# One stage for latent keys, values and queries, with the norm weights folded into the down projections

## The chip, the cores and the metric

One core of one Trainium2 chip runs the whole program. The time is device microseconds of one execution, and the median of three runs is what two versions are compared by. The core has five engines with instruction queues of their own: TensorE (PE; its weight loads are PEld), VectorE (DVE), ScalarE (ACT), GpSimd (POOL) and SyncE (SP, which here only issues DMAs). An engine takes its instructions strictly in order and waits on semaphores for the others.

## The reference, cut to what matters

The program is two layers of a small transformer (512 tokens and 16 meta tokens, width 1024, all in float32), followed by two further layers of other kinds. The change is in the second layer's latent attention, between the first layer's mixture of experts and the attention itself:

```python
def shared_latent_kv(h, kv_norm, w_dkv, kv_lat_norm, w_uk, w_uv, cos, sin):
    c = jnp.einsum('bld,dr->blr', rmsnorm(h, kv_norm), w_dkv)       # 1024 -> 256 + 64
    c_kv = rmsnorm(c[..., :KV_LORA_RANK], kv_lat_norm)
    k_rope = apply_rope(c[..., KV_LORA_RANK:], cos, sin)
    k_nope = jnp.einsum('blr,rhd->blhd', c_kv, w_uk)
    v = jnp.einsum('blr,rhd->blhd', c_kv, w_uv)
    return k_nope, k_rope, v

def mla_mixer(hn, w_dq, q_norm, w_uq, ...):                          # hn = rmsnorm(h, b_norm)
    cq = rmsnorm(jnp.einsum('bld,dr->blr', hn, w_dq), q_norm)        # 1024 -> 384
    q = jnp.einsum('blr,rhd->blhd', cq, w_uq)                        # 8 heads x (128 + 64)
    q_nope = q[..., :QK_NOPE_DIM]
    q_rope = apply_rope(q[..., QK_NOPE_DIM:], cos[:, None, :], sin[:, None, :])
```

Both norms are taken of the same `h`; they differ only in the weight that each column is multiplied by (`kv_norm`, `b_norm`).

## The kernel before

**Arithmetic.** Every large product is made of three matmuls of rounded halves (`products`, lines 105 to 109): the high part of one operand with both parts of the other, and the low part with the high one. An operand is split by a copy on ScalarE that rounds (the "high" part) and a subtraction on VectorE (the "low" part).

**Weights.** All weights come in chunks of up to 128 x 2048, in one list. SyncE loads them in that order into raw buffers (four outside the experts, `load_chunk`), each as soon as the buffer's last user is done; ScalarE (`split_high`, line 246) and VectorE (`split_low`, line 260) split them into one of three pairs of split buffers, once the chunk that had the pair is used up. The list is mixed with chunks for the third part of the network, the "ada" pieces (`load_list`): 1 MB each, two of them make one `ada_rows` of 16 matmuls on TensorE, read from the raw buffer without a split, followed by `ada_pick` on VectorE. Six of these pieces, (1,0) to (1,5), stand behind the first experts' last chunk and ahead of the latent stage's first.

**The stages here** are `moe` 0, `latent`, `query`, `attend`. A stage starts on an engine once all engines have ended the stage ahead; only `route`, `latent` and `enter` start without that.

`latent`: GpSimd fetches the experts' rows (`yc`, five DMAs, four of 1 MB). Per tile t of 128 tokens (four, and a fifth of the 16 meta tokens), VectorE adds the two expert rows (`combine_vector`), ScalarE takes the root of the mean square, VectorE multiplies by its reciprocal and the row of weights (line 339), TensorE transposes (line 357), ScalarE and VectorE split the result into `x_high` and `x_low`. Three `ada_rows` stand between these transposes. Then the chunks c, c+1 and c+2 are split and TensorE makes `c` (five tiles of 24 matmuls, 320 wide); ScalarE copies it out (`c_rows`), the norm over 256 and the rotation by position are made on VectorE for all tiles; ten small transposes and five of the rotary part follow (lines 999 and 1000), split into `ck_high`, `ck_low`, `k_rope_high`, `k_rope_low`; then come the keys (96 matmuls of 264) and the values (60 of 512).

`query`: `h` is normed, transposed and split a second time, with the row `b_norm`; `cq` (96 matmuls of 384), its norm over 384 (line 1201), transposes (line 1136), split; the rotary queries (36 matmuls of 512), their rotation on VectorE (six operations a tile, lines 948 to 956, two buffers in turn), transposes (line 1151), split; the plain queries `q_nope`, eight heads of nine matmuls of 512, copied out by ScalarE (line 1189).

`attend` begins on TensorE with ten matmuls whose result nobody reads (line 1292), then the first scores, then ten more (line 1296).

## Time and profile before

| | us |
|---|---|
| median of three runs | 2884.91 |
| lowest and highest of them | 2884.13, 2894.32 |
| the profiled execution's own time | 2893.18 |
| its span in the trace | 2891.4 |
| granted TensorE clock, mean over the span | 0.927 of full |

A granted clock of 1.00 is 2.4 GHz, one of 0.50 is 1.2 GHz; a value between is a stretch with some of both. A DMA's landing, a wait or a busy time of the trace belongs to the one profiled execution, which took 8.27 us more than the median.

### The profile page before, as it was taken

The page shows a single profiled execution, that of the slowest core. Times are in us where ns is not written, and L with a number is a line of the kernel's source. Part 1 is how long each engine was busy: PE and PEld are TensorE (multiplying, and loading weights), DVE is VectorE, ACT ScalarE, POOL GpSimd, SP SyncE. Part 2 cuts the span into 40 slices and gives each one's busy share as a digit, 9 for nine tenths or more (in the row PEclk, how much of TensorE's full clock was granted, in tenths as well). Part 3 has the DMA queues.
Part 4 walks back from the last instruction along what each step waited for, and adds up shares of the span by engine and source line. Part 5 has one row for each costly group of instructions (what it writes and reads, how often), then busy time and mean ns, then how long its engine had stood idle before and what let it go on. Part 6 is the DMA issues. An engine that isn't in the chain of part 4 may idle for free.

```text
span 2891.4 us, 31119 instructions
## 1 busy us (share of the span) xinstructions
PE 2566.1 (89%) x11522; PEld 2033.9 (70%) x11522; DVE 1874.9 (65%) x2237; ACT 1366.2 (47%) x1901; POOL 211.8 (7%) x221
## 2 busy tenths in 40 slices
PE   5879999778996999997987889989798998899997
PEld 2668888566775888884665667778666666688886
DVE  4679999644635999985863756545774664644356
ACT  2258888533633888884522322123332563332321
POOL 1022222100001222211000000000000000000000
PEclk9789999888997999998996889999998899899999
DMA  7379991431013999615220245443211002222230
GB/s 259 112 300 365 367 361 69 174 115 46 16 44 131 369 365 367 251 63 212 73 73 29 80 165 199 149 142 116 74 60 44 1 1 102 80 102 102 73 110 29
DMA packets 100374, 418.57 MB, mean 145 GB/s; under 512 B 25737, under 2 KB 26081, under 8 KB 60785
## 3 DMA queue, kind: packets, MB, share of 16 engines
q1 hardware_dynamic: 70976, 373.27, 35.5%
q0 software_dynamic: 29248, 43.32, 4.2%
q8 instruction: 93, 1.52, 0.2%
q14 instruction: 57, 0.46, 0.1%
HBM read 484.91 MB, written 48.76 MB: 185 GB/s over the span
## 4 chain that ended last, share of the span: by engine, by line
PE 74%; DVE 15%; ACT 5%; issue 3%; DMA 2%; POOL 0%; SPq 0%; DVEq 0%; ACTq 0%; POOLq 0%
PE psum L107 22%; PE psum L108 21%; PE psum L109 21%; PE psum L742 2%; DVE w_low L260 2%; ACT w_high L246 1%; PE psum L1532 1%; DVE ada_sum L1564 1%; PE psum L486 1%; PE psum L357 1%; DVE rg_in L2181 1%; DMA raw<-in_ada 1%; DVE gla_head L2181 1%; PE psum L759 1%; DMA rows<-in_rows 1%
## 5 line engine op out<-in xcount | busy, mean ns | idle before, releaser
L260 DVE TENSOR_TENSOR w_low<-raw,w_high 128x2048 fp32r<-128x2048 f32 (+1 forms) x216 | 485.3, 2258 | 260.2 <-ACT w_high L246 247.9
L246 ACT ACTIVATE w_high<-raw 128x2048 fp32r<-128x2048 f32 (+1 forms) x216 | 405.7, 1886 | 317.6 <-PE psum L109 304.2
L107 PE MATMUL psum<-x_high,w_high 128*128 128x512 f32 x848 | 348.4, 411 | 39.6 <-DVE w_low L260 25.3
L108 PE MATMUL psum<-x_high,w_low 128*128 128x512 f32 x848 | 339.6, 400 | 0.0
L109 PE MATMUL psum<-x_low,w_high 128*128 128x512 f32 x848 | 337.8, 398 | 0.0
L107 PE MATMUL psum<-w_high,mlp_high 128*128 128x512 f32 x512 | 205.1, 401 | 27.5 <-DVE mlp_low L932 11.5
L107 PEld LDWEIGHTS psum<-x_high,w_high 128*128 128x128 f32 x848 | 160.6, 189 | 87.2 <-issue 40.4
L109 PE MATMUL psum<-w_low,mlp_high 128*128 128x512 f32 x512 | 205.3, 401 | 0.0
L108 PE MATMUL psum<-w_high,mlp_low 128*128 128x512 f32 x512 | 204.9, 400 | 0.0
L107 PE MATMUL psum<-w_high,xg_high 128*128 128x512 f32 x480 | 195.7, 408 | 6.2 <-DVE xg_low L853 6.2
L108 PEld LDWEIGHTS psum<-x_high,w_low 128*128 128x128 f32 x848 | 160.5, 189 | 43.7 <-issue 6.4
L260 DVE TENSOR_TENSOR w_low<-raw_extra,w_high 128x2048 fp32r<-128x2048 f32 x78 | 177.8, 2289 | 18.5 <-ACT w_high L246 13.4
L109 PE MATMUL psum<-w_low,xg_high 128*128 128x512 f32 x480 | 189.4, 394 | 0.0
L108 PE MATMUL psum<-w_high,xg_low 128*128 128x512 f32 x480 | 189.3, 394 | 0.0
L109 PEld LDWEIGHTS psum<-x_low,w_high 128*128 128x128 f32 x848 | 160.5, 189 | 39.3 <-issue 1.1
L246 ACT ACTIVATE w_high<-raw_extra 128x2048 fp32r<-128x2048 f32 x78 | 149.7, 1919 | 15.0 <-PE psum L109 15.0
L107 PEld LDWEIGHTS psum<-w_high,mlp_high 128*128 128x128 f32 x512 | 98.9, 193 | 50.3 <-ACT mlp_high L928 17.1
L107 PE MATMUL psum<-w_high,x_high 128*128 128x512 f32 (+5 forms) x272 | 104.3, 383 | 33.5 <-DVE w_low L260 16.5
L893 POOL DMA_INDIRECT expert_rows<-yb,table x80 | 92.5, 1156 | 549.4 <-PE psum L742 444.9
L928 ACT ACTIVATE mlp_high<-mlp_square 128x512 fp32r<-128x512 f32 x64 | 40.5, 632 | 190.1 <-DVE mlp_square L2533 190.1
L1532 PE MATMUL psum<-raw,condition 128*128 128x512 f32 x192 | 95.0, 653 | 31.7 <-DMA raw<-in_ada 30.2
L853 DVE TENSOR_TENSOR xg_low<-psum,xg_high 128x1024 fp32r<-128x1024 f32 x80 | 98.0, 1224 | 30.1 <-ACT xg_high L799 21.6
(542 smaller groups left out, 5410.4 us busy)
## 6 DMA issues: line engine op xcount, KB each, us to landing
raw<-in_moe SPq DMA_DIRECT2D x138, 1024.0 KB
raw_extra<-in_moe SPq DMA_DIRECT2D x102, 1024.0 KB
raw<-in_mlp SPq DMA_DIRECT2D x64, 1024.0 KB
raw<-in_ada SPq DMA_DIRECT2D x48, 1024.0 KB
rows<-in_rows POOLq DMA_DIRECT2D x20, 512.0 KB, 4.7
raw<-in_evin SPq DMA_DIRECT2D x10, 1024.0 KB
raw<-in_foxqk SPq DMA_DIRECT2D x8, 1024.0 KB
xn_rows<-xn_tiles POOLq DMA_DIRECT2D x9, 512.0 KB, 3.0
```

The source lines that it names most:

```text
L107: pe.matmul(out, ah, bh, start=first, stop=False)
L108: pe.matmul(out, al, bh, start=False, stop=False)
L109: return pe.matmul(out, ah, bl, start=False, stop=last)
L246: act.activation(k.WH[k.W_AT[c]][:, 0:w], k.RAW[k.RAW_AT[c]][:, 0:w], ACT.Copy).then_inc(*k.A.step("high", c))
L260: dve.tensor_tensor(wl[:, 0:w], k.RAW[k.RAW_AT[c]][:, 0:w], wh[:, 0:w].bitcast(F32), ALU.subtract).then_inc(*k.V.step("low", c))
L357: mm = pe.transpose(k.PS[:, b, i * P:(i + 1) * P], xn, const(k, "ident"))
L742: mm = pe.transpose(flat(k, f * P, f * P + P), k.XG[:, j % XG_SLOTS, f * P:(f + 1) * P], const(k, "ident"))
L853: dve.tensor_tensor(k.XGL[j % 2][:, :, :].rearrange("p a b -> p (a b)"), flat(k, 0, D), k.XGH[j % 2][:, :, :].rearrange("p a b -> p (a b)" ...
L893: pool.indirect_dma_start(k.y_d[:, :], bass.IndirectOffsetOnAxis(ap=k.TAB[:, 2 * j + 1:2 * j + 2], axis=0), k.YB[:, j % 2, :], None, bound ...
L928: act.activation(dst, src, ACT.Copy).then_inc(*k.A.step(*label))
L1532: mm = pe.matmul(k.PS[:, bank, :], k.CS[:, f:f + 1].to_broadcast([P, P]), w[:, i * ADA_COLS:(i + 1) * ADA_COLS], start=(f == 0), stop=(f = ...
L2181: f(*a, **b).then_inc(*V.step())
```

## The change

The stage `query` is gone; `latent` makes keys, values and queries.

- One normalisation: `h` is multiplied by the reciprocal root alone, without a row of weights, by a `tensor_scalar`. Its transposed halves serve both down projections.
- The weights `kv_norm` and `b_norm` go into the four chunks of the down projections when these are split (`GAINED`): four ScalarE copies with a scale per partition instead of one copy, four VectorE operations (raw times scale minus high) instead of one subtraction. Only the 1280 used columns of the key chunks are split, not 2048. The scales are columns, transposed with the other gain rows in the first stage (11 rows instead of 9); the two rows are no longer loaded as rows of 128 partitions.
- The chunks are in the order of the new stage: both down projections, keys, rotary queries, values, plain queries.
- The six ada pieces stand behind c and c+1 in the list of loads; c and c+1 are split before the norm.
- TensorE's order: `c`, `cq`, the transposes of both, keys, rotary queries, values, transposes of rotary queries, plain queries. `cq` keeps banks 0 to 3 of PSUM, `c` and its transposes 4 to 7. The rotated rows have four buffers instead of two. ScalarE copies out all values.
- ScalarE splits two chunks of `attout`'s weights in this stage, c+9 and c+10, instead of one.
- `ada_pick` of the first vector writes its unused product to PSUM instead of SBUF.

```diff
@@ load_list
-        follow.setdefault(k.MOE0[n // 6] + 3 * NBLK - 1, []).append((1, n))
+        follow.setdefault((k.FIRST[("latent",)] + 1, k.MOE0[1] + 3 * NBLK - 1)[n // 6], []).append((1, n))
@@ split_high
+        if c in k.GAINED:
+            g, f0, w = k.GAINED[c]
+            for i in range(4):
+                act.activation(wh[:, i * w:(i + 1) * w], raw[:, i * w:(i + 1) * w], ACT.Copy,
+                               scale=k.GAINC[:, g, f0 + i:f0 + i + 1]).then_inc(*k.A.step("high", c))
+            continue
@@ split_low
+                dve.scalar_tensor_tensor(out=wl[:, part], in0=k.RAW[k.RAW_AT[c]][:, part], scalar=k.GAINC[:, g, f0 + i:f0 + i + 1],
+                                         in1=wh[:, part].bitcast(F32), op0=ALU.mult, op1=ALU.subtract).then_inc(*k.V.step("low", c))
@@ norm_vector
+            dve.tensor_scalar(xn, k.H[:, t, :], k.RS[:, t:t + 1], None, ALU.mult).then_inc(*k.V.step(name, "xn", t))
@@
+LATENT_ORDER = (0, 1, 4, 5, 2, 6, 3, 7, 8)
@@ latent_tensor
+    for q in range(2):
+        wh, wl = chunk_pair(k, pe, c + 2 + q)
+        for t in range(XT):
+            for f in range(4):
+                w = slice(f * QR, f * QR + QR)
+                mm = products(pe, k.PS[:, t, 0:QR], k.XH[:, 4 * q + f, t * P:(t + 1) * P], k.XL[:, 4 * q + f, t * P:(t + 1) * P],
+                              wh[:, w], wl[:, w], q == 0 and f == 0, q == 1 and f == 3)
...
+    for t in range(XT):
+        pe.wait_ge(*k.after("cq normed", t))
+        for f in range(3):
+            mm = pe.transpose(k.PS[:, t, f * P:(f + 1) * P], k.CQN[:, t, f * P:(f + 1) * P], const(k, "ident"))
@@ latent_scalar
+    split_high(k, act, c + 1)
     norm_scalar(k, act, "latent", range(XT + 1), "pair", k.SQ, "combined", 0)
-    split_high(k, act, c + LOOK)
+    split_high(k, act, c + 2)
...
+    split_high(k, act, c + 9)
+    for h in range(HEADS):
+        if h == 4:
+            split_high(k, act, c + 10)
+        act.wait_ge(*k.after("qn", h))
+        act.activation(k.QN[:, h, :], k.PS[:, latent_bank(LATENT_QN + h), :], ACT.Copy).then_inc(*k.A.step("qn out", h))
@@ latent_vector
+    split_low(k, dve, c + 1)
+    norm_vector(k, dve, "latent", range(XT + 1), "pair", None, combined)
...
+    split_low(k, dve, c + 4)
     dve.wait_ge(*k.after("cq root"))
@@ stage_list
-    return ([("pool",), ("route", 0, XT + 1), ("moe", 0), ("latent",), ("query",), ("attend",), ("attout",),
+    return ([("pool",), ("route", 0, XT + 1), ("moe", 0), ("latent",), ("attend",), ("attout",),
@@ chunk_list
+        if st[0] == "latent":
+            new = [new[i] for i in LATENT_ORDER]
```

SyncE's queue between the last chunk of the first experts and the latent stage (`in_kv`, `in_q` and `in_wo` are weights, `in_ada` the ada pieces, `raw_49` to `raw_52` the four raw buffers), before:

```order
L231 DMA raw_50<-in_moe 128x2048
L218 DMA raw_51<-in_ada 128x4x512
L218 DMA raw_52<-in_ada 128x4x512
L218 DMA raw_49<-in_ada 128x4x512
L218 DMA raw_50<-in_ada 128x4x512
L218 DMA raw_51<-in_ada 128x4x512
L218 DMA raw_52<-in_ada 128x4x512
L234 DMA raw_49<-in_kv 128x2048
L234 DMA raw_50<-in_kv 128x2048
```

and now:

```order
L232 DMA raw_50<-in_moe 128x2048
L235 DMA raw_51<-in_kv 128x2048
L235 DMA raw_52<-in_kv 128x2048
L219 DMA raw_49<-in_ada 128x4x512
L219 DMA raw_50<-in_ada 128x4x512
L219 DMA raw_51<-in_ada 128x4x512
L219 DMA raw_52<-in_ada 128x4x512
L219 DMA raw_49<-in_ada 128x4x512
L219 DMA raw_50<-in_ada 128x4x512
L235 DMA raw_51<-in_q 128x1536
L235 DMA raw_52<-in_q 128x1536
```

Two weight chunks have moved ahead of the six ada pieces, and pieces (1,2) and (1,3) now take the buffers of these two chunks, so they are issued once VectorE has split them.

TensorE's queue behind the last matmul of `c` (320 wide), before:

```order
L108 MATMUL psum<-w_high_55,x_low 16x320
L109 MATMUL psum<-w_low_58,x_high 16x320
L999 MATMUL psum<-const,c_norm 128x128 x2
L1000 MATMUL psum<-const,k_rope_rows 128x128
L999 MATMUL psum<-const,c_norm 128x128 x2
```

and now behind the last matmul of `cq` (384 wide):

```order
L108 MATMUL psum<-w_high_54,x_low 128x384
L109 MATMUL psum<-w_low_57,x_high 128x384
L1084 MATMUL psum<-const,c_norm 128x128 x2
L1085 MATMUL psum<-const,k_rope_rows 128x128
L1084 MATMUL psum<-const,c_norm 128x128 x2
```

The same transposes stand in the same order, but behind `cq`, which is made in between. Where they end, at the tile of the meta tokens, TensorE's queue now goes on so:

```order
L1085 MATMUL psum<-const,k_rope_rows 128x128
L1084 MATMUL psum<-const,c_norm 128x16 x2
L1085 MATMUL psum<-const,k_rope_rows 128x16
L1089 MATMUL psum<-const,cq_norm 128x128 x12
L107 MATMUL psum<-ck_high,w_high_55 128x264
L108 MATMUL psum<-ck_high,w_low_58 128x264
```

The twelve transposes of the queries' latents (`cq_norm`) have moved in between the keys' transposes and the keys' matmuls (264 wide).

ScalarE's queue at the end of the queries, `q_nope` being their copies and `q_high` the first instruction of `attend`, before:

```order
L928 ACTIVATE q_rope_high<-psum 128x4x128 x4
L246 ACTIVATE w_high_53<-raw_49 128x1536
L1189 ACTIVATE q_nope<-psum 128x512 x4
L246 ACTIVATE w_high_55<-raw_50 128x2048
L1189 ACTIVATE q_nope<-psum 128x512 x4
L928 ACTIVATE q_high<-q_nope 128x512
```

and now:

```order
L949 ACTIVATE q_rope_high<-psum 128x4x128 x4
L254 ACTIVATE w_high_55<-raw_50 128x2048
L1208 ACTIVATE q_nope<-psum 128x512 x4
L254 ACTIVATE w_high_53<-raw_51 128x2048
L1208 ACTIVATE q_nope<-psum 128x512 x4
L949 ACTIVATE q_high<-q_nope 128x512
```

A second weight split (`raw_51`, chunk c+10) stands between the copies of heads 0 to 3 and those of heads 4 to 7. It waits until TensorE has used up chunk c+8 in the same pair of buffers, that is, until all heads are made.

## Rows read from the trace of the kernel before

**Rows 1.** the page's part 4, shares of the chain that ended last

```profile
PE 74%; DVE 15%; ACT 5%; issue 3%; DMA 2%; POOL 0%; SPq 0%; DVEq 0%; ACTq 0%; POOLq 0%
```

**Rows 2.** windows: length; busy (count) of PE, PEld, DVE, ACT, POOL; clock, DMA share, GB/s

```profile
549.00:558.70 9.70, 2.12 (x5) 0.58 (x4) 2.59 (x3) 0.20 (x1) 3.37 (x7) 0.84 0.99 391
594.20:614.60 20.40, 20.37 (x120) 18.84 (x120) 4.60 (x3) 2.84 (x5) 0.00 (x0) 0.86 0.34 116
614.60:622.90 8.30, 0.03 (x1) 0.07 (x1) 4.58 (x14) 5.06 (x13) 0.00 (x0) 0.64 0.00 0
622.90:627.40 4.50, 3.19 (x15) 2.75 (x15) 4.31 (x11) 2.37 (x10) 0.00 (x0) 0.50 0.29 79
627.40:640.30 12.90, 12.83 (x94) 12.86 (x95) 3.03 (x7) 3.02 (x8) 0.00 (x0) 0.87 0.09 35
640.30:654.60 14.30, 14.30 (x64) 10.21 (x62) 6.54 (x7) 5.72 (x8) 0.00 (x0) 1.00 0.36 128
654.60:667.60 13.00, 6.02 (x34) 5.52 (x33) 9.99 (x15) 9.38 (x19) 0.00 (x0) 0.76 0.01 2
667.60:686.40 18.80, 18.80 (x98) 18.49 (x96) 3.14 (x3) 3.84 (x9) 0.00 (x0) 0.89 0.18 57
686.40:692.10 5.70, 2.74 (x14) 2.12 (x13) 4.67 (x8) 4.21 (x8) 0.00 (x0) 0.70 0.00 0
692.10:702.10 10.00, 10.00 (x38) 8.08 (x38) 5.95 (x15) 0.00 (x0) 0.00 (x0) 0.83 0.31 105
702.10:708.90 6.80, 2.69 (x18) 2.21 (x17) 5.88 (x15) 1.68 (x3) 0.00 (x0) 0.77 0.00 0
708.90:727.30 18.40, 18.40 (x73) 14.45 (x71) 5.38 (x5) 7.85 (x10) 0.00 (x0) 0.90 0.30 97
```

**Rows 3.** chain of waits in order of time: start us, us, what

```profile
549.17 9.49 DMA yc<-expert_rows
...
562.88 1.30 DVE h L920
...
566.76 1.30 DVE xn L339
...
588.76 0.89 PE psum L357 x8
...
591.78 2.30 DVE w_low L260
```

**Rows 4.** timeline, VectorE: start us, us, what [idle before it]

```profile
555.86 2.60 DVE L920 SCALAR_TENSOR_TENSOR h<-yc,gate,h 128x1024 f32<-128x1024 f32 x2 [14.69 <-DMA yc<-expert_rows]
...
618.34 2.07 DVE L1094 SCALAR_TENSOR_TENSOR c_norm<-c_rows,rs,param 128x256 f32<-128x256 f32 x5
...
625.03 0.42 DVE L932 TENSOR_TENSOR ck_low<-psum,ck_high 128x256 fp32r<-128x256 f32 x1
...
687.60 2.19 DVE L1201 SCALAR_TENSOR_TENSOR cq_norm<-psum,rs,param 128x384 f32<-128x384 f32 x4
689.71 1.75 DVE L260 TENSOR_TENSOR w_low<-raw,w_high 128x1536 fp32r<-128x1536 f32 x1
...
696.00 0.42 DVE L948 TENSOR_TENSOR rotate_c<-psum,const 128x256 f32<-128x256 f32 x1 [2.68 <-PE psum L109]
```

**Rows 5.** groups by shape, VectorE, 1290 to 1360 us

```profile
L1743 DVE TENSOR_SCALAR h<-h,rs 128x1024 f32<-128x1024 f32 x4 | 3.0, 753 | 0.1
```

**Rows 6.** timeline, SyncE's queue: first issue, us to the last

```profile
535.86 15.66 SPq L218 DMA_DIRECT2D raw<-in_ada  x3
...
574.85 14.26 SPq L234 DMA_DIRECT2D raw<-in_kv  x4
```

**Rows 7.** timeline, ScalarE and TensorE at the stage's end

```profile
719.55 1.91 ACT L246 ACTIVATE w_high<-raw 128x2048 fp32r<-128x2048 f32 x1
...
727.46 0.60 ACT L1189 ACTIVATE q_nope<-psum 128x512 f32<-128x512 f32 x1 [1.50 <-PE psum L109]
...
728.10 2.55 PE L1292 MATMUL psum<-q_rope_high 128*128 128x512 f32 x10 [0.69 <-ACT q_nope L1189]
```

More of the change, by code:

```diff
@@ L316, in norm_vector @@
 def norm_vector(k, dve, name, tiles, mode, gain, earlier=None):
-    dve.wait_ge(*k.after("row", gain))
+    if gain:
+        dve.wait_ge(*k.after("row", gain))
     def lows(t):
@@ L962, in table3, with key_col, latent_bank, latent_freed @@
     return k.CONST[:, at + t0 * h:at + (t0 + nt) * h].rearrange("p (t f) -> p t f", t=nt)
+def key_col(t):
+    return (META + t * P, P) if t < XT else (0, META)
+LATENT_KV = 2 * HEADS
+LATENT_QR = LATENT_KV
+LATENT_V = LATENT_QR + XT
+LATENT_TURN = LATENT_V + 2 * (XT + 1)
+LATENT_QN = LATENT_TURN + XT
+def latent_bank(n):
+    return 4 + n % 4 if n < 8 else n % 8
+def latent_freed(n):
+    if n < LATENT_KV:
+        return "kv out", n
+    if n < LATENT_V:
+        return "qr rotated", n - LATENT_QR
+    if n < LATENT_TURN:
+        return "kv out", n - XT
+    if n < LATENT_QN:
+        return "qr lo", n - LATENT_TURN
+    return "qn out", n - LATENT_QN
+def kv_place(k, r):
+    n = r if r < LATENT_KV else r + XT
+    if r < 2 * HEADS:
+        h, s = divmod(r, 2)
+        return k.KT[:, h, s * KHALF:(s + 1) * KHALF], k.PS[:, latent_bank(n), 0:KHALF]
+    t, half = divmod(r - 2 * HEADS, 2)
+    if t < XT:
+        return k.VAL[:, t, half * HALF:(half + 1) * HALF], k.PS[:, latent_bank(n), :]
+    return k.H[0:META, XT, half * HALF:(half + 1) * HALF], k.PS[0:META, latent_bank(n), :]
 def latent_tensor(k, pe, *_):
     c = k.FIRST[("latent",)]
+    def bank(n):
+        if 4 <= n < 8:
+            pe.wait_ge(*k.after(*latent_freed(n - 4)))
+        elif 8 <= n < 12:
+            pe.wait_ge(*k.after("cq lo", n - 8))
+        elif n >= 12:
+            pe.wait_ge(*k.after(*latent_freed(n - 8)))
+        return latent_bank(n)
     for t in range(XT + 1):
@@ L1099, in latent_vector @@
     dve.tensor_copy(k.KRD[:, :, ROPE:P], k.KRD[:, :, 0:ROPE]).then_inc(*k.V.step("k turned by position"))
-    split_low(k, dve, c + 3)
-    for t in range(XT + 1):
-        c0, n = key_col(t)
-        dve.wait_ge(*k.after("kr", t))
-        low(k, dve, k.KRL[:, c0:c0 + n], k.PS[:, t % 4, 2 * P:2 * P + n], k.KRH[:, c0:c0 + n], "kr lo", t)
-        src = k.PS[:, t % 4, 0:2 * P].rearrange("p (a c) -> p a c", a=2)[:, :, 0:n]
-        low(k, dve, k.CKL[:, :, c0:c0 + n], src, k.CKH[:, :, c0:c0 + n], "ck lo", t)
@@ L1192, in query_vector @@
-def query_vector(k, dve, *_):
-    c = k.FIRST[("query",)]
-    norm_vector(k, dve, "query", range(XT), "pair", "b_norm")
-    split_low(k, dve, c + LOOK)
+    split_low(k, dve, c + 4)
     dve.wait_ge(*k.after("cq root"))
@@ L1218, in query_vector @@
         cols = slice(t * P, (t + 1) * P)
[L1219 to L1220 removed]
+        low(k, dve, k.QRTL[:, :, cols], turned_queries(k, t), k.QRTH[:, :, cols], "qr lo", t)
     dve.wait_ge(*k.after("qn", 3))
[L1222 removed]
+    split_low(k, dve, c + 9)
+    dve.wait_ge(*k.after("qn", 7))
+    split_low(k, dve, c + 10)
 def unit(u):
@@ L2942, in place_rest @@
     k.CKL = k.at("ck_low", [P, 2, KEYS], k.end, F32R)
-    k.CQN = k.at("cq_norm", [P, XT, QR], k.SCR)
+    k.CQN = k.at("cq_norm", [P, XT, QR], va)
+    k.SQQ = k.at("cq_squares", [P, QR], k.end)
     k.QRTH = k.at("q_rope_high", [P, HEADS // 2, SEQ], k.XHAT, F32R)
@@ L3032, in place_rest @@
     k.OL = k.at("fox_low", [P, DK, SEQ], fv, F32R)
-SCALAR = {"pool": pool_scalar, "route": route_scalar, "moe": moe_scalar, "latent": latent_scalar, "query":
-          query_scalar, "attend": attend_scalar, "attout": attout_scalar, "enter": enter_scalar,
+SCALAR = {"pool": pool_scalar, "route": route_scalar, "moe": moe_scalar, "latent": latent_scalar, "attend": attend_scalar, "attout": attout_scalar, "enter": enter_scalar,
           "even_in": even_in_scalar,
@@ L3063, in chunk_list @@
     out, moe0, overflow = [], [], {}
-    names = {"pool": ["a_w"], "latent": ["kv"], "query": ["q"], "attout": ["wo"], "even_in": ["evin", "evz"],
+    names = {"pool": ["a_w"], "latent": ["kv", "q"], "attout": ["wo"], "even_in": ["evin", "evz"],
              "even_out": ["evout"], "fox_in": ["foxqk", "foxf", "foxv"], "fox_out": ["foxg", "foxout"]}
@@ L3098, in program @@
     k.high_next = k.low_next = 0
+    c = first.get(("latent",), 0)
+    k.GAINED = {c: (9, 0, CWID), c + 1: (9, 4, CWID), c + 2: (10, 0, QR), c + 3: (10, 4, QR)} if c else {}
     k.xn_d = nc.dram_tensor("xn_rows", ((XT + 1) * P, D), F32, kind="Internal").ap()
@@ L3246, in rows @@
                 k.row_next += 1
-                if ("row done", ROWS[r]) not in marks and marks.get("complete"):
+                if ROWS[r] not in COLUMNS_ONLY and ("row done", ROWS[r]) not in marks and marks.get("complete"):
                     break
-                if r >= ROW_SLOTS:
-                    pool.wait_ge(*k.after("row done", ROWS[r - ROW_SLOTS]))
+                if ROWS[r] in COLUMNS_ONLY:
+                    continue
+                prev = next((p for p in range(r - ROW_SLOTS, -1, -ROW_SLOTS) if ROWS[p] not in COLUMNS_ONLY), None)
+                if prev is not None:
+                    pool.wait_ge(*k.after("row done", ROWS[prev]))
                 pool.dma_start(k.ROWB[:, r % ROW_SLOTS, :], dram["rows"][r]).then_inc(
```

267 lines of the change are left out of this document (128 added, 139 removed).

## The prediction, made before the changed kernel ran

> **What bounds the kernel now.** I read the shares of the chain that ended last first: TensorE holds 74% of it, VectorE 15% [rows 1], so time is won where TensorE stands still or runs at half clock. Then I cut the latent and query stages into windows at the places where TensorE changes work [rows 2]. Each row is one piece of work or one pause; the clock behind the busy times tells how much of it ran at 2.4 GHz. Where TensorE is busy throughout, length times clock is the length at full clock: `c` 20.4 x 0.86 = 17.5 us, `cq` 18.8 x 0.89 = 16.7, keys 12.9 x 0.87 = 11.2, values 14.3, rotary queries 10.0 x 0.83 = 8.3, plain queries 18.4 x 0.90 = 16.6. The rest is pauses: 8.3 and 4.5 us around the keys' norm and transposes, 13.0 for the second norm of `h`, 5.7 for the queries' norm, 6.8 for the rotated queries, each followed by a stretch at half clock. DMA moves 128 GB/s or less in all of these, so no transfer sets their end. Last I followed the chain of waits from the experts' rows to the first matmul of `c` [rows 3], and VectorE's own queue [rows 4].
>
> **The front of the stage.** Before, `c` starts at 594.2, 4.5 us after the last transposes of the norm (588.76 + 0.89 = 589.65), because ScalarE and VectorE split three chunks after the norm (VectorE from 591.78) [rows 3]. Now c and c+1 are split before it. ScalarE is free after the experts' last rows, and VectorE has 14.69 us of idle time ahead of the first `h` [rows 4], which hides two splits of about 2 us each; were that cover gone, 4.6 us of VectorE would stand on the path. Four operations on 320 columns cost what the c_norm and cq_norm rows say of such shapes: 2.07/5 = 0.41 us at 256 columns, 2.19/4 = 0.55 at 384, so 1.9 to 2.2 us a chunk on VectorE [rows 4], against 2.30 for one subtraction [rows 3]; I cost it at nothing. The multiplication into `xn` falls from 1.30 us [rows 3] to 0.75, the row of a `tensor_scalar` of this shape [rows 5]; three of the five stand on the chain (at 561.49, 566.76 and 579.46; one is shown): 1.6 us. So `c` could start at 588.1.
>
> Against it stands a collision. SyncE issued three ada pieces in the 15.66 us from 535.86 [rows 6], two of them at about the time when GpSimd fetches the experts' rows; now four fall there, (1,2) and (1,3) when VectorE has split c and c+1, (1,4) and (1,5) right behind. Between 549.0 and 558.7 the DMA engines are full, 391 GB/s x 9.7 us = 3.8 MB [rows 2]; 2.1 MB of it are the first two tiles of rows, landed at 549.17 + 9.49 = 558.66 [rows 3], a share of 55%. Going on at this share the third tile (1.05 MB) lands 4.9 us later, at 563.5, and its addition was due at 562.88 [rows 3], now half a microsecond earlier: 1.2 us late. The bounds: nothing, if rows come first; 2.1 MB / 391 GB/s = 5.4 us if both extra pieces come first. I take 1.0. `c` starts at 589.1: **5.1 us gained**.
>
> **`c` and `cq` at full clock.** TensorE no longer pauses between the ada matmuls, the last transposes and `c`, so `c` takes 17.5 us instead of 20.4: **2.9**. `cq` follows at once, 16.7 instead of 18.8: **2.1**. Its second half waits for c+3, which can be split only once `c` has used its buffers; ScalarE and VectorE need some 4 us for it and the first half of `cq` is 8 us long, so it is covered. The keys' norm and rotation (8.3 us of pause before) lie under the same 16.7 us.
>
> **The remaining pause.** Behind `cq` come the queries' squares, root and norm, then both sets of halves. Before, that was 5.7 us for the queries [rows 2], 1.75 of it for a weight split [rows 4] that is now done earlier: 4.0 us. To this come the keys' halves: ten subtractions on VectorE (0.42 us for the long ones [rows 4], 2.5 us in all) now queued behind `cq_norm` and ahead of `cq_low`, the fifth tile's transposes behind the first of them, and fifteen transposes. I take 4.0 + 3.2 = 7.2 us. Bounds: 4.0, if the keys' halves cost nothing; 8.3 + 4.5 + 5.7 = 18.5, if both chains run as long as before, one after the other. Before, the pauses here were 8.3 + 4.5 + 13.0 + 5.7 = 31.5: **24.3**. The clock will fall in this pause, as it does in the three like it (0.64, 0.76, 0.70 [rows 2]), so the keys take 12.9 or 13.0 as before: **-0.1**.
>
> **Rotary queries.** No pause ahead of them: 8.3 instead of 10.0, **1.7**. Their rotation, six operations of 0.42 us a tile [rows 4], runs under the values' 14.3 us, with a weight split between: 4 x 2.6 + 1.8 = 12.2, the first tile beginning 2 us into 8.3 + 14.3. Values need the banks of the third and fourth tile some 9 us into their work, when these are done. Sixteen transposes then take some 2.1 us at full clock (eight took 0.89 us of the chain [rows 3]; I add a little for waits), not 6.8: **4.7**. The plain queries, with no pause ahead, 16.6 instead of 18.4: **1.8**.
>
> **The end of the stage.** Before, `attend` began 0.7 us after the last copy's product [rows 7]. Now ScalarE must split c+10 between the copies, and that split waits for TensorE's last head: 1.91 us [rows 7], then four copies of 0.6 us or a little less [rows 7]; VectorE's half of the split runs beside these. `attend` starts 4.4 us after the last head instead of 0.8: **-3.6**. Behind the waiting split stand the copies of heads 4 to 7, and all of `attend` waits for them. The pause also lets the clock fall: the ten unread matmuls took 2.55 us [rows 7] and double at 1.2 GHz, and the first scores are slower. Bounds 0 and 5 us (both sets of ten); I take **-2.0**, since about one set is needed to bring the clock back. By the Trainium skill, page "TensorE: Matmul & The Clock Gate", section "Part 1: The HAM clock gate", the low clock is what TensorE falls back to whenever it has been idle, and work has to release it; the windows above agree (0.64 to 0.76 in each pause). By that rule the warm-up matmuls behind a new pause run slow at first.
>
> Elsewhere two 512 KB rows are not loaded and two short DMAs are added in the first stage, where GpSimd waits anyway: nothing. The second split of `attout` weights was not on the path there: nothing.
>
> **Sum:** 5.1 + 2.9 + 2.1 + 24.3 - 0.1 + 1.7 + 4.7 + 1.8 - 3.6 - 2.0 = 36.9 us. The profiled execution took 2893.18 us, 8.3 more than the median, so the changed one would be near 2856 by this execution, and **2848 us** against the median of 2884.91.
>
> **Rivals.**
> A. *The experts' rows come late.* Four pieces of ada compete with them; if the extra 2.1 MB go ahead, the front loses 5.4 instead of 1.0: 2852. For it: a DMA share of 0.99 [rows 2]; against: the third tile has slack. By the Trainium skill, page "DMA: Bandwidth & Descriptors", section "Queues, rings and completion order", an engine with work on several queues takes them in turn, a packet at a time. By that rule, the rows would get about half; the 55% above agrees.
> B. *The two norms' chains add up.* The pause behind `cq` is nearer 18 us, with VectorE's queue (cq_norm, keys' halves, queries' halves) as the bound: 11 us less gained, 2859. Against: the keys' norm has no input from `cq`.
> C. *The front does not move*, because the splits of c and c+1 come too late for VectorE's gap: 5.1 + 2.9 are lost, 2856. Against: the chunks are asked for before the last experts' work.
> D. *More is gained*: the pause behind `cq` is 4.0 us and the clock holds at the end: 5 us more, 2843.
> E. *Slower.* TensorE stays at half clock in the merged stage, its many short waits never letting it rise. The work at full clock is 17.5 + 16.7 + 11.2 + 14.3 + 8.3 + 16.6 = 84.6 us and would take that much more: about 2930. It decides against the change once some 37 us of this work that I count at full clock run at half. Against: before, every one of the six pieces came back to full clock, with means of 0.83 or more [rows 2].
> F. *No change*: the chain runs elsewhere, through DMA. Against: 128 GB/s or less.
>
> **How the numbers follow.** The forecast 0.62, A 0.11, B 0.10, C 0.05, D 0.09, E 0.02, F 0.01. The likeliest case has 2843 to 2853 from its own bounds. With A, C, D and most of B, and the 10 us between the three runs of before, the range is 2838 to 2861. About 0.5% (14 us) is what a measurement of this kernel can tell from no change; B's full size is still a gain of 26. Faster 0.96, within 0.5% 0.02, slower 0.02.
>
> **What would show it.** Right: the first 320-wide matmul less than 1 us behind the last transposes of the norm, with the clock at 1.00; no 1024-wide norm after that; `cq` directly behind `c`; one pause of about 7 us before the 264-wide matmuls, and none before the transposes of rotated queries; a pause of about 4 us before `attend`. Wrong: a wait of `h` for the rows after the second tile; a pause within `cq` for its second chunk; values waiting for a rotation; or a stage whose clock is below 0.8. The total would be wrong too if `attend` itself, which I take as unchanged, ran otherwise.

## The result, and the profile after

The changed kernel takes 2847.6 us (median of 2852.62, 2851.97, 2843.23 and 2840.11) against 2888.9 us of the kernel before on the same chip: ratio 0.9854, 95% interval [0.9832, 0.9876], 41 us less. The forecast was 2848. In the profiled executions the span fell from 2891.4 to 2850.9 us, 40.5 less.

Two marks that both kernels have make the change measurable in the trace alone: the moment when GpSimd issues the copy of the experts' rows (`yc`), and VectorE's first maximum of scores in `attend`. From VectorE's timeline, before and after (start us, us, what):

```profile
731.73 0.31 DVE L1381 TENSOR_REDUCE tops<-psum 128x1 f32<-128x144 f32 x1 [1.49 <-PE psum L1266]
```

```profile
691.96 0.31 DVE L1439 TENSOR_REDUCE tops<-psum 128x1 f32<-128x144 f32 x1 [3.96 <-PE psum L1324]
```

From GpSimd's timeline, the issue of the rows, before and after:

```profile
548.60 1.67 POOL L911 DMA_DIRECT2D yc<-expert_rows  x3 [1.65 <-DMA expert_rows<-yb,table]
```

```profile
549.68 2.68 POOL L932 DMA_DIRECT2D yc<-expert_rows  x5 [1.66 <-DMA expert_rows<-yb,table]
```

731.73 - 548.60 = 183.13 us before, 691.96 - 549.68 = **142.28 us after: 40.85 less**. The whole difference lies in this stretch; the rest of these two executions is equally long to 0.4 us. A second profile of the unaltered changed kernel gave 142.29, where single total times of one kernel differ by 10 us and more. Between kernels the stretch is less sharp than these two values suggest: the start of `c` moves by some 0.7 us and the clock behind a pause by 1.3 us without an edit (last section), so a difference under 2 us is read from its pieces and not from the sum. All comparisons below use it and call it "the stretch".

The windows of the changed kernel, cut where TensorE changes work (columns as in [rows 2]):

```profile
549.68:587.60 37.92, 24.80 (x80) 13.42 (x78) 26.64 (x50) 12.87 (x26) 3.24 (x6) 0.77 0.85 307
587.60:605.20 17.60, 17.60 (x124) 16.37 (x121) 4.09 (x15) 4.05 (x10) 0.00 (x0) 1.00 0.31 107
605.20:621.90 16.70, 16.70 (x99) 16.67 (x98) 8.79 (x18) 8.86 (x23) 0.00 (x0) 1.00 0.28 95
621.90:628.80 6.90, 4.24 (x29) 3.98 (x27) 5.61 (x17) 4.17 (x16) 0.00 (x0) 0.82 0.00 0
628.80:641.10 12.30, 12.30 (x99) 12.30 (x98) 7.77 (x12) 6.80 (x12) 0.00 (x0) 0.96 0.26 87
641.10:649.40 8.30, 8.30 (x38) 6.84 (x37) 6.40 (x15) 1.49 (x1) 0.00 (x0) 1.00 0.36 126
649.40:663.40 14.00, 14.00 (x63) 10.20 (x62) 7.06 (x14) 6.72 (x11) 0.00 (x0) 1.00 0.37 125
663.40:665.60 2.20, 2.20 (x19) 2.07 (x18) 1.18 (x2) 2.20 (x5) 0.00 (x0) 1.00 0.39 164
665.60:681.50 15.90, 15.80 (x70) 12.73 (x68) 3.60 (x4) 4.09 (x7) 0.00 (x0) 1.00 0.17 58
681.50:686.00 4.50, 0.00 (x1) 0.03 (x1) 2.29 (x1) 3.92 (x6) 0.00 (x0) 0.82 0.07 27
686.00:691.96 5.96, 5.96 (x19) 4.78 (x20) 1.31 (x2) 2.01 (x5) 0.00 (x0) 0.57 0.53 180
```

In order: the front, `c`, `cq`, the one remaining pause, keys, rotary queries, values, transposes of rotated queries, plain queries, the new pause ahead of `attend`, the unread matmuls and first scores. Where before only the values had a clock of 1.00 and the other products 0.83 to 0.90 [rows 2], six of these seven pieces of work are at 1.00, and the keys at 0.96. The last two rows are the price: a pause, and behind it a stretch at 0.57.

In place of [rows 3], the chain of waits through the front, and then through the stage's end:

```profile
550.25 7.92 DMA yc<-expert_rows
558.19 1.30 DVE h L941
...
560.90 0.76 DVE xn L360
...
586.96 0.87 PE psum L378 x8
587.83 0.15 PE psum L107
```

```profile
681.49 1.92 ACT w_high L254
...
683.60 2.30 DVE w_low L276
...
686.00 4.60 PE psum L1350 x10
```

The `c` matmuls (0.15 us each, full clock) stand directly behind the norm's last transposes; the rows landed 7.92 us after the end of their first issue instead of 9.49. At the end the chain goes through both halves of the second split of `attout`'s weights (ScalarE at L254, VectorE at L276, done at 685.90), and the ten unread matmuls take 4.60 us instead of 2.55 [rows 7]. ScalarE's timeline there shows who stands behind whom:

```profile
675.16 2.04 ACT L1208 ACTIVATE q_nope<-psum 128x512 f32<-128x512 f32 x4
681.49 1.91 ACT L254 ACTIVATE w_high<-raw 128x2048 fp32r<-128x2048 f32 x1 [4.30 <-PE psum L109]
683.31 2.04 ACT L1208 ACTIVATE q_nope<-psum 128x512 f32<-128x512 f32 x4
```

ScalarE sits idle for 4.30 us with copies of finished heads waiting behind the split, then makes split and copies when TensorE has nothing left to do. The copies are done at 685.35, half a microsecond ahead of VectorE's half of the split, so it is the split itself on which `attend` waits here, with the copies close behind.

The shares of the chain are 75% TensorE, 15% VectorE, 5% ScalarE, as in [rows 1]: shares over the span do not show a change of 1.5%.

### The profile page after: what moved, and what is told of

Its sections match the earlier page's. It is cut to its first block, busy times and chain, and to the rows that moved or that the text cites. A ratio compares the mean times of both kernels' runs of the same rounds, so it can differ in the third digit from the quotient of the medians.

```text
span 2850.9 us, 31032 instructions
## 1 busy us (share of the span) xinstructions
PE 2549.3 (89%) x11490; PEld 2026.4 (71%) x11490; DVE 1859.7 (65%) x2228; ACT 1359.4 (48%) x1898; POOL 213.2 (7%) x221
## 4 chain that ended last, share of the span: by engine, by line
PE 75%; DVE 15%; ACT 5%; issue 3%; DMA 1%; SPq 0%; DVEq 0%; POOL 0%; ACTq 0%; POOLq 0%
PE psum L107 22%; PE psum L108 21%; PE psum L109 21%; PE psum L763 3%; DVE w_low L276 2%; PE psum L1590 1%; ACT w_high L254 1%; DVE ada_sum L1622 1%; PE psum L507 1%; DVE rg_in L2239 1%; DMA raw<-in_ada 1%; PE psum L378 1%; DVE gla_head L2239 1%; PE psum L780 1%; DVE residual_tmp L1840 1%
## 5 line engine op out<-in xcount | busy, mean ns | idle before, releaser
L276 DVE TENSOR_TENSOR w_low<-raw,w_high 128x2048 fp32r<-128x2048 f32 (+1 forms) x212 | 477.6, 2262 | 272.4 <-ACT w_high L254 251.4
L254 ACT ACTIVATE w_high<-raw 128x2048 fp32r<-128x2048 f32 (+1 forms) x212 | 399.4, 1890 | 328.6 <-PE psum L109 315.1
L276 DVE TENSOR_TENSOR w_low<-raw_extra,w_high 128x2048 fp32r<-128x2048 f32 x78 | 177.7, 2288 | 18.6 <-ACT w_high L254 15.2
L254 ACT ACTIVATE w_high<-raw_extra 128x2048 fp32r<-128x2048 f32 x78 | 149.2, 1912 | 15.1 <-PE psum L109 15.1
L949 ACT ACTIVATE mlp_high<-mlp_square 128x512 fp32r<-128x512 f32 x64 | 40.5, 632 | 188.9 <-DVE mlp_square L2591 188.9
```

The source lines that it names most:

```text
L254: act.activation(wh[:, 0:w], raw[:, 0:w], ACT.Copy).then_inc(*k.A.step("high", c))
L276: dve.tensor_tensor(wl[:, 0:w], k.RAW[k.RAW_AT[c]][:, 0:w], wh[:, 0:w].bitcast(F32), ALU.subtract).then_inc(*k.V.step("low", c))
L949: act.activation(dst, src, ACT.Copy).then_inc(*k.A.step(*label))
```

## The experiments

Each kernel is the changed one with the edit shown, unless the text says otherwise. Ratios are to the kernel before on the same chip.

| kernel | median us | ratio, 95% | the stretch, us |
|---|---|---|---|
| before | | 1 | 183.13 |
| changed | 2847.6 | 0.9854 [0.9832, 0.9876] | 142.28 |
| changed, again | 2848.3 | 0.9841 [0.9816, 0.9866] | 142.29 |
| one split | 2842.5 | 0.9818 [0.9787, 0.9849] | 135.94 |
| keys in cq | 2841.4 | 0.9823 [0.9802, 0.9845] | 137.28 |
| both | 2833.6 | 0.9804 [0.9782, 0.9826] | 131.14 |
| norm exposed | 2854.8 | 0.9894 [0.9841, 0.9947] | 150.50 |
| front back | 2852.5 | 0.9864 [0.9818, 0.9910] | 149.30 |
| before, one norm | 2871.7 | 0.9946 [0.9926, 0.9967] | 173.36 |
| rows first | 2839.1 (one run) | | 139.95 |
| first row | 2851.4 (one run) | | 142.63 |
| all | 2829.0 | 0.9790 [0.9768, 0.9813] | 130.68 |

### The changed kernel again

> The changed kernel unaltered, beside the three below on one chip. 2847.6 us, ratio 0.985 to the kernel before; what differs from this between its runs is the measure of what the three can tell by their total times.

Measured: 2848.3 us, the stretch 142.29. Its six runs went from 2835.9 to 2851.4; why, is told in the last section.

### One split less at the end

```diff
@@ latent_scalar
     for h in range(HEADS):
-        if h == 4:
-            split_high(k, act, c + 10)
@@ latent_vector
-    dve.wait_ge(*k.after("qn", 7))
-    split_low(k, dve, c + 10)
```

> The second split of attout's weights (chunk c+10) is left to attout itself; nothing else changes. Theory: it alone makes the pause ahead of attend, since the copies of heads 4 to 7 stand behind it on ScalarE. Then the warm-up matmuls begin less than 1 us behind the last head's matmul instead of about 4.5, at full clock, and the first maximum of scores comes about 3.6 us after the stage's end as before instead of 6.0: 3.6 + 2.4 = 6.0 us less, 2841.6. Rival 1: only the pause goes, the first scores wait for q_high and the halves of the first head on VectorE in any case: 3.6 us less or nothing. Rival 2: the split comes back in attout, whose second chunk is then late: 2 us lost there, 4 us less in all.

Measured: the stretch is 6.3 us shorter, 135.94. ScalarE's timeline and TensorE's row behind it:

```profile
674.72 3.02 ACT L1206 ACTIVATE q_nope<-psum 128x512 f32<-128x512 f32 x6
...
681.00 0.60 ACT L1206 ACTIVATE q_nope<-psum 128x512 f32<-128x512 f32 x1 [1.44 <-PE psum L109]
681.71 0.63 ACT L949 ACTIVATE q_high<-q_nope 128x512 fp32r<-128x512 f32 x1
```

```profile
681.65 2.56 PE L1346 MATMUL psum<-q_rope_high 128*128 128x512 f32 x10 [0.69 <-ACT q_nope L1206]
```

The copies follow the heads, the pause is 0.69 us, the unread matmuls take 2.56 us again, and the first maximum comes 4.3 us after the last head's product instead of 10.5 (4.3 before). Rival 1 falls: the clock is regained too. For rival 2 the trace has the last addition of `attout` on VectorE (`h<-h,psum`, at 838.79 in the changed kernel and at 831.46 here). From the first maximum of scores to there it is 146.83 us in the changed kernel and 146.18 here, where 2 us more were to be seen: `attout` gives nothing back. (The kernel before has 145.95, so the changed one lost another 0.9 us behind the stretch's end.) The run takes out the waiting split as a whole; what its place ahead of the four copies costs by itself was not tried.

### The keys' transposes within cq

`ck_high` and `ck_low` get a place that `cq` does not read (behind the rotated rows), and the fifth tile's small transposes use the free columns of the first tile's bank, so that all five stand in one block. The transposes of `cq_norm`, their halves and some copies move in between the keys on all three engines (`CQ_TURN` is 6). The core of it:

```diff
@@ latent_tensor
         for t in range(XT):
+            if q and t == 2:
+                turn_keys()
...
     for r in range(LATENT_KV):
+        if r == CQ_TURN:
+            turn_queries()
@@ latent_scalar
     for t in range(XT):
+        if t == 2:
+            act.wait_ge(*k.after("ck turned", XT))
+            for u in CK_ORDER:
+                c0, n = key_col(u)
+                high(k, act, k.CKH[:, :, c0:c0 + n], ck_pair(k, u, n), "ck hi", u)
+                high(k, act, k.KRH[:, c0:c0 + n], ck_turned(k, u, 2, n), "kr", u)
         act.wait_ge(*k.after("cq", t))
@@ latent_vector
+    for t in CK_ORDER:
+        c0, n = key_col(t)
+        dve.wait_ge(*k.after("kr", t or XT))
+        low(k, dve, k.KRL[:, c0:c0 + n], ck_turned(k, t, 2, n), k.KRH[:, c0:c0 + n], "kr lo", t)
+        low(k, dve, k.CKL[:, :, c0:c0 + n], ck_pair(k, t, n), k.CKH[:, :, c0:c0 + n], "ck lo", t)
     dve.wait_ge(*k.after("cq root"))
...
-    for t in range(XT + 1):
-        c0, n = key_col(t)
-        b = 4 + t % 4
-        dve.wait_ge(*k.after("kr", t))
...
```

> The keys' transposes move into cq, behind the second of its last four tiles (their inputs are ready at 615.5 us and cq reaches that point at 617.7), their halves get a place of their own instead of x_high's, the keys' matmuls stand directly behind cq, and the transposes of cq_norm behind the sixth of the sixteen keys' groups. Theory: the 6.9 us pause behind cq is a matter of order alone and goes, but for about 3 us of transposes that TensorE now makes at full clock: the keys start at about 623.6 instead of 628.8 and end at 636.1 instead of 641.1: 5 us less, 2842.6. Rival: VectorE becomes the bound of the keys' stretch (keys' copies 3.4, cq_norm 2.2, cq_low 2.5, two splits 4.0 us: 12.2 in 12.5 us), TensorE waits for banks and for cq_low, and the pause only moves: 2 us less or none.

Measured: the stretch is 5.0 us shorter, 137.28. TensorE's timeline, then VectorE's:

```profile
616.07 0.38 PE L1059 MATMUL psum<-const,c_norm 128*128 128x128 f32 x2
...
622.07 0.28 PE L107 MATMUL psum<-ck_high,w_high 128*128 128x264 f32 x1
...
626.44 1.47 PE L1066 MATMUL psum<-const,cq_norm 128*128 128x128 f32 x12
```

```profile
623.21 0.18 DVE L1261 RECIPROCAL rs<-rt 128x4 f32<-128x4 f32 x1 [2.21 <-ACT rt L1196]
```

The keys begin 74.3 us after the rows' issue instead of 79.1, right behind `cq`; the twelve transposes run at full clock (1.47 instead of 2.82 us) between two groups of keys, and TensorE does not stop. VectorE, the rival's bound, even has 2.21 us idle ahead of `cq_norm`. So the pause that was left in the changed kernel was one of order. Of the 5.0 us, 4.0 are there at the end of the keys, though `c` began 0.25 us later (38.2 us after the rows' issue); the last one comes at the stage's end, where the unread matmuls took 3.92 us instead of 4.60 behind the same 4.60 us pause.

### Both

> Both edits: one split fewer at the end, and the keys' transposes within cq. Theory: the two pauses lie apart, so the gains add up: 6.0 + 5.0 = 11 us less than the changed kernel, 2836.6. Rival: they do not add up, because the clock or ScalarE's queue in the stage's end eats part of it: 2841 or more.

Measured: 131.14, 11.15 us shorter; 2833.6 us in all, ratio 0.9804 [0.9782, 0.9826], where the changed kernel has 2848.3 on this chip. The gains add up but for the microsecond of clock that both edits claim at the end: 6.3 + 5.0 - 1.0 = 10.3, and the rest is an earlier start of `c` (37.3 us after the rows' issue, 38.2 in the run with the keys in `cq`), which came and went without an edit (last section).

### The keys' norm exposed

```diff
@@ latent_scalar
     split_high(k, act, c + 3)
+    act.wait_ge(*k.after("cq", XT - 1))
     for t in range(XT + 1):
```

> The changed kernel with one wait added: ScalarE begins the squares of the keys' norm only when cq is finished, so that nothing of the keys' norm and rotation lies under cq; both chains now stand one after the other behind it (rival B of the prediction, made on purpose). Theory: c's squares and root take 622 to 625, c_norm, rotation and the weight split on VectorE to 631.8, the keys' transposes lie under that split, then cq_norm, the keys' halves and cq's transposes follow: the keys start at about 636.4 instead of 628.8. The stretch from the first fetch of the experts' rows to the first maximum of scores, 142.3 us in the changed kernel, becomes 150 to 151; 2856 in all. That is what the cover of cq is worth. Rival: the chains add up in full to the 18.5 us of the upper bound, keys at 640.4: 154. Other rival: VectorE's and ScalarE's queues overlap them so well that it costs 3 us or less: 145.

Measured: 150.50, 8.2 us longer. From its chain of waits:

```profile
609.89 0.18 PE psum L109
610.09 0.52 ACT c_norm L1163 x2
...
620.23 2.19 DVE cq_norm L1243 x4
...
623.50 2.75 PE psum L1089 x12
```

From the last product of `cq` at 610.07 to the keys' first at about 626.2 it is 16 us, between the expected 14.5 and the upper bound of 18.5. (The stretch shows 8.2 of the 9 us because `c` began 0.7 us earlier here.) Both rivals, 154 and 145, are ruled out. So 9 us of the keys' norm and rotation lie under `cq` in the changed kernel; rival B was a real price, but only for an order in which the cover is missing.

### The front as before

```diff
@@ load_list
-        follow.setdefault((k.FIRST[("latent",)] + 1, k.MOE0[1] + 3 * NBLK - 1)[n // 6], []).append((1, n))
+        follow.setdefault(k.MOE0[n // 6] + 3 * NBLK - 1, []).append((1, n))
@@ latent_scalar
-    split_high(k, act, c + 1)
@@ latent_vector
-    split_low(k, dve, c + 1)
```

> The changed kernel with its front as before: the six ada pieces ahead of c and c+1 in the list of loads, and c and c+1 split behind the norm instead of ahead of it. Theory: c starts 4.5 us later, at half clock (2.8 us more for c), and the experts' rows land 9.5 instead of 7.9 us after their issue, since an ada piece is then issued 1 us ahead of them and not 0.8 us behind: 1.6 us. The stretch from the rows' issue to the first maximum of scores becomes 142.3 + 8.9 = 151.2; 2856 in all. Rival: the landing of the rows has nothing to do with the order of the pieces, and stays at 7.9: 149.6. Other rival: the splits are hidden behind the ada matmuls between the transposes in either place, as rival C had it: 142 to 144.

Measured: 149.30, 7.0 us longer instead of 8.9. The chain of waits and TensorE's timeline:

```profile
549.00 9.94 DMA yc<-expert_rows
...
591.28 0.94 DVE w_low L272 x2
592.35 0.60 PE psum L107
```

```profile
633.23 0.29 PE L1084 MATMUL psum<-const,c_norm 16*128 16x16 f32 x2 [2.67 <-DVE ck_low L953]
...
633.51 1.53 PE L1089 MATMUL psum<-const,cq_norm 128*128 128x128 f32 x12
```

and TensorE's timeline of the changed kernel at the place of the last two rows:

```profile
626.02 0.29 PE L1084 MATMUL psum<-const,c_norm 16*128 16x16 f32 x2 [2.66 <-DVE ck_low L953]
...
626.31 2.82 PE L1089 MATMUL psum<-const,cq_norm 128*128 128x128 f32 x12
```

The rows take 9.94 us again, so their landing does hang on the order of the pieces, and `c` starts 43.9 us after their issue instead of 37.9: 6.0, the two terms of the theory (4.5 + 1.6). `c` takes 20.1 instead of 17.6 us (`cq` follows at 612.40). Then 1.4 us come back: in the pause behind `cq` the clock did not fall, so that the twelve transposes took 1.53 us and not 2.82, though TensorE stood still for as long as in the changed kernel (2.67 and 2.66 us). The theory held for the front and missed this.

### The kernel before without its second norm

The edit to the kernel before:

```diff
@@ query_tensor
-    norm_tensor(k, pe, "query", range(XT))
     for t in range(XT):
-        for half in range(2):
-            pe.wait_ge(*k.after("query", "out", t, half))
@@ query_scalar
-    norm_scalar(k, act, "query", range(XT), "pair", k.SQ)
@@ query_vector
-    norm_vector(k, dve, "query", range(XT), "pair", "b_norm")
@@ place_rest
-    k.CKH = k.at("ck_high", [P, 2, KEYS], k.XHAT, F32R)
+    k.CKH = k.at("ck_high", [P, 2, KEYS], kt - 4 * KEYS * 4, F32R)
```

> The kernel before with its second norm, transposition and split of h left out: the queries are computed from the halves made with kv_norm, so their values are not the reference's; the keys' halves are placed elsewhere so that x_high survives, and the keys' transposes use five banks. Theory: the 13.0 us pause goes but for the start of the stage, and cq runs at full clock, 16.7 instead of 18.8: 13.0 + 2.1 = 15.1 us less than before, so that the stretch from the rows' issue to the first maximum of scores falls from 183.1 to 168; the rest of the gain, 25.7 us, is not the second norm's but the order's. Rival: the norm covered the stage's start and the splits of cq's chunks, and 5 us of them appear in its place: 173.

Measured: 173.36, 9.8 us less than before, where 15.1 or, by the rival, 10 were expected; in total ratio 0.9946. The windows, from `c` to the end of the values, `cq` with the pause ahead of it, and the rest:

```profile
585.50:648.84 63.34, 51.80 (x291) 45.72 (x291) 23.12 (x41) 18.68 (x43) 0.00 (x0) 0.82 0.23 79
648.84:666.65 17.81, 16.98 (x96) 16.69 (x96) 2.44 (x2) 3.23 (x7) 0.00 (x0) 1.00 0.18 60
666.65:712.91 46.26, 38.22 (x155) 29.89 (x156) 23.20 (x42) 16.43 (x27) 0.00 (x0) 0.85 0.21 69
```

The middle one was 13.0 + 18.8 = 31.8 us before [rows 2]: 14.0 gained, with `cq` at full clock and only 0.8 us left of the pause. The rival was not the reason for the rest: my edit of the keys' halves cost 2.9 us in the first window (60.4 before, from 594.2 to 654.6), 0.9 was lost in the last and 0.3 in the front. So the second norm, with its clock, was worth 14 of the 40.9 us. The other 27 are what is left by subtraction: the order of the work, but for 1.6 us of the cheaper `xn` (1.30 to 0.76 us, three on the chain).

### The rows first

```diff
@@ load_chunk
     if not isinstance(c, int):
+        if c == (1, 2):
+            sync.wait_ge(*k.after("rows", 0, 1))
```

> The changed kernel with one wait on SyncE: ada piece (1,2), and with it all behind it, is issued only when the experts' rows of the second tile have landed, so that no ada piece is issued beside the first two tiles of rows. It measures what the collision costs in the changed kernel. Theory: it still costs 2 us there. The two tiles, 2.1 MB at 377 GB/s, land 5.6 us after their issue instead of 7.9, the first xn comes 2.4 us earlier; the pieces (1,2) and (1,3) then land by about 567.4 instead of being there at 568.4, and give 1 us or less back: the stretch from the rows' issue to the first maximum of scores is 140 to 141.3 instead of 142.3. Rival: the pieces set the end of the front, not the rows: what the rows win the pieces lose, 142.3 or up to 145.

> The same wait on the first tile of rows alone. Theory: the first tile lands 2.8 us after its issue instead of 4.6, but the second, which xn waits for through VectorE's queue, lands within 0.9 us of the 7.9 of before; 141.4 to 142.3. Rival: as above, a delay of the pieces shows instead: more than 142.5.

Measured: 139.95 with the wait on the second tile, 142.63 on the first. The chain of the first of them:

```profile
538.54 5.05 DMA yc<-expert_rows
543.62 1.29 DVE h L943
...
547.43 1.28 ACT L303
```

The first tile took as long as ever (5.1 us; 5.2 in the changed kernel), not 2.8; the second was there when VectorE asked for it. SyncE, which waits for just this landing, issues piece (1,2) at 546.15, 7.6 us after the rows' issue; the theory had 5.6 behind it, and the changed kernel 8.5. `c` starts 36.9 us after the rows' issue. Against 37.9 that would be 1.0, but two executions of other kernels with the front unaltered had 37.2 and 37.3 (norm exposed, both), and they are of the same kind as this one in the first routing stage (last section); against these it is 0.4. The other 1.3 us of the 2.3 are the pause behind `cq`, passed at full clock here (twelve transposes in 1.53 us), which has nothing to do with the wait. The theory's total came out right for a reason that it did not name: the collision costs the changed kernel about half a microsecond, not 2. With the wait on the first tile alone `c` starts 38.1 us after the issue, among the 37.9 to 38.2 of the kernels of its kind with the front unaltered: no gain, and 142.63 is too close to 142.5 to call it the rival's loss. With the rows there, ScalarE's load of a function table (1.28 us, the last row above) stands on the chain next.

### All three edits

> The three edits together: one split of attout's weights in the stage, the keys' transposes within cq, and the ada pieces (1,2) to (1,5) issued behind the landing of the second tile of rows. Theory: the three places lie apart. The first two gave 131.1 us for the stretch from the rows' issue to the first maximum of scores; the wait made c start 36.9 us after the rows' issue instead of 37.9: 130.1. In all about 2832, against 2848 of the changed kernel. Rival: what the wait gave beyond the 1.0 us at c's start (139.95 in place of 142.3 in all) was a gain of its own and comes again: 128.8.

Measured: 130.68, and 2829.0 us, ratio 0.9790 [0.9768, 0.9813], the shortest stretch of all; in total time the intervals of this kernel and of the one with two edits overlap. `c` starts at 36.9 us as forecast, 0.4 ahead of the kernel with two edits, and 0.46 is the gain. The rival (128.8) falls.

## Why the prediction was right

The stretch came out 40.9 us shorter, for 36.9 forecast. Term by term, from [rows 2] and the windows above:

| term | forecast | measured |
|---|---|---|
| front (45.6 to 37.9 us) | 5.1 | 7.7 |
| `c` | 2.9 | 2.8 |
| `cq` | 2.1 | 2.1 |
| pauses (31.5 to 6.9) | 24.3 | 24.6 |
| keys | -0.1 | 0.6 |
| rotary queries | 1.7 | 1.7 |
| values | 0 | 0.3 |
| rotated transposes | 4.7 | 4.6 |
| plain queries | 1.8 | 2.5 |
| end: pause and clock | -5.6 | -6.0 |

- **The pauses and the clock.** The step that carries the forecast held. The remaining pause was worked out at 7.2 us and took 6.9, with other parts than I added: of the keys' halves only the first pair stands on the chain (0.5 us, not 2.5), and the twelve transposes of `cq_norm` at half clock (2.75 us) fill the place. The run with the norm exposed shows the cover (9 us), the one without the second norm its 14 us.
- **The end of the stage.** The loss was foreseen with its cause, the split that waits for the last head, and the run with one split shows it alone: 6.3 us, for 5.6 forecast and 6.0 measured. That the copies of heads 4 to 7 would be last was not quite so: they ended at 685.35 and VectorE's half of the split, which I had beside them, at 685.90. The clock's part was 2.3 us, for 2.0. (The clocks of the pauses before go from 0.50 to 0.77 [rows 2], not from 0.64 to 0.76 as I wrote.)
- **The front** was mis-sized by 2.6 us. I took 1.0 for a collision of the rows with the ada pieces. The rows landed 1.6 us sooner than before instead. SyncE's timeline has one piece issued 0.9 us ahead of the rows and one behind them before, and all four behind them now, since they wait for VectorE's splits (from 550.48 to 553.37, the rows at 549.68):

```profile
547.72 0.37 SPq L218 DMA_DIRECT2D raw<-in_ada  x1
```

```profile
550.48 12.45 SPq L219 DMA_DIRECT2D raw<-in_ada  x4
```

So more pieces fell beside the rows than before, as I had counted, and the rows still came sooner. In the 8.51 us from the rows' issue to the landing of their second tile the changed kernel moves 321 GB/s, 2.7 MB, 2.1 MB of them the two tiles: 77%, not the 55% from which I went on. The DMA view tells the two queues apart, GpSimd's with the rows (q0) and SyncE's with the pieces (q1): packets, MB, share of the engines. In the first 3.0 us from the rows' issue, before (nothing moves for the rows) and after (nothing for the pieces):

```profile
q1 hardware_dynamic: 391, 0.80, 81.5%
```

```profile
q0 software_dynamic: 54, 0.44, 49.8%
```

And later, when both queues move data, after (554.86 to 558.19):

```profile
q0 software_dynamic: 150, 1.10, 78.6%
q1 hardware_dynamic: 146, 0.30, 23.0%
```

Before, from 555.86 to 558.68, it is 126 packets and 0.90 MB for the rows' queue, 126 and 0.26 MB for the pieces'.

So the piece issued ahead had the engines to itself before, and the first packets of rows move only 3.3 to 3.6 us after the rows' issue; now they move 1.1 to 1.4 us after it. The run with the front as before has the late start again (3.5 to 3.8 us) and the late landing with it. That is the step that I had wrong: 55% was no share at which two queues settle, but the mean over a start in which the rows had nothing, and what is issued ahead of the rows counts, not how many pieces fall beside them. The rule of the Trainium skill that I set beside it (page "DMA: Bandwidth & Descriptors", section "Queues, rings and completion order", queues served in turn, a packet at a time) fits the later windows, with 126 packets to 126 and 150 to 146. But I had read it as half of the bytes. The packets of rows carry some 7 KB here and those of the pieces 2 KB, so the rows have 78% of the bytes while both queues work. Why the rows' first packets do not take their turn while the piece ahead is under way was not shown.
- **Keys and plain queries**, 0.7 us each. For the keys I let the clock fall in the pause as in the three like it. In the changed kernel it did, but was full again 0.8 us into the keys; in two other runs it never fell. For the plain queries some 0.5 us are the place of my cuts: their first matmul stands at 664.79, 0.8 us ahead of the cut, and before at 708.57, 0.3 ahead; the transposes' term is the larger by as much. The rest was not explained.
- **That the number was hit to half a microsecond is partly luck.** The sum was 4 us too small, and the median of the kernel before moved up by 4 us: the result has a fourth run of it, 2892.80, beside the three that were shown (2884.9 and 2888.9). The gain was 41, within the range that I gave.
- Of the rivals, A (rows late) is refuted by the landing after 7.92 us, C by the first `c` matmul behind the transposes (VectorE was idle for 2.55 us between the splits and the first `h`), E by the clock column, F by the 40.9 us. B and D were prices of real things that did not come: B's order had to be built to be seen. D's "clock holds at the end" comes with one split less.

## What to carry to other kernels

A norm or a rotation between two products is hidden (9 us of it here) if a product that does not need it is put in between; look for such a product before looking for a faster norm. When weight splits are scheduled into an engine's queue by hand, ask of each what it waits for, and who stands behind it: a split that waits for the end of the stage makes a pause and a half-clock start, 6.3 us here for 1.9 us on ScalarE and 2.3 on VectorE that the next stage could take in without loss. When a transfer is urgent, look at what is issued on another queue just ahead of it, and not only at how much will run beside it. In a program whose total varies by 10 us between executions, measure between two marks inside the trace.

## What the runs showed of the hardware that I had not expected

**Identical code, two clocks, 10 us.** On the chip of the first experiments the runs of one kernel lie on levels some 10 us apart: the changed kernel's had 2835.9 and 2836.0, then 2847.6 to 2851.4; the kernel before 2884.4 to 2885.2, then 2892.7 to 2897.4. Not all do: the six runs with one split go from 2826.0 to 2851.1 with values between. The traces show one source. In the first routing stage, some 400 us ahead of the experiments' edits, TensorE's router matmuls ran at 1.2 GHz in one profile and at 2.4 GHz in another. The window from 111 to 120 us of the changed kernel, and of the one with the norm exposed:

```profile
111.00:120.00 9.00, 9.00 (x45) 9.00 (x44) 1.77 (x5) 3.12 (x7) 1.06 (x2) 0.50 0.29 117
```

```profile
111.00:120.00 9.00, 9.00 (x75) 8.28 (x75) 1.61 (x9) 6.20 (x8) 0.53 (x1) 1.00 0.19 75
```

45 matmuls in one, 75 in the other. GpSimd's first gather of rows for the experts then stands at 157.3 us and at 146.2. Of twelve profiles seven were of the first kind (gather at 155 to 157) and five of the second (145 to 147), with both kinds among kernels that do not differ in that stage. No kernel was profiled in both kinds, so that this is what parts the run times is inferred. The kind also goes with the start of `c`: 37.9 to 38.2 us after the rows' issue in the five profiles of the first kind with `c` and c+1 split early, 37.2 and 37.3 in the two of the second whose loads are not held back. The Trainium skill, page "TensorE: Matmul & The Clock Gate", section "Part 1: The HAM clock gate", says that how many matmuls start out at the low clock varies from run to run of one kernel, and puts the penalty under 1% of a typical kernel's span. It speaks of the start of a kernel; here the variation stands 111 us into the program. Its size agrees: 10 us are 0.35%, which is still more than most single edits of this study gained. What decides between the two levels was not tried.

**The same pause, with and without a fall.** Behind `cq` TensorE waits 2.66 us for the fifth tile in the changed kernel and 2.67 us in the one with the front as before; the next twelve transposes took 2.82 us in one and 1.53 in the other. Of the other kernels with this pause, the one with the rows first had 1.53 too, and the one with the first row 2.45. And behind the same 4.60 us ahead of `attend` the ten unread matmuls took 4.60 or 4.61 us in six profiles and 3.92 in the one with the keys in `cq`. A term for the clock behind a pause is good to one microsecond here, no better.

**A copy in four pieces on ScalarE.** The split of a query chunk with a scale per partition, four times 384 columns, took 2.12 us, while one copy of 1536 columns takes 1.48 in the same kernel; VectorE's four operations took 2.20 instead of 1.76. It was hidden here, and would be 0.6 us of ScalarE per chunk where it is not.
